# One more column group of forgetting attention is computed inside its loop, and the groups there start and end one third later

## What is computed

```python
def _fox(q, k, v, f_logit, f_bias):
    ...
    log_f = jax.nn.log_sigmoid(f_logit.astype(jnp.float32) + f_bias.astype(jnp.float32))
    cum = jnp.cumsum(log_f, axis=1)
    ...
    def attend(args):
        qb, cq, idx = args
        q_pos = idx * Q_BLOCK + jnp.arange(Q_BLOCK)
        sc = jnp.einsum('bqhd,bkhd->bhqk', qb, k, preferred_element_type=jnp.float32) * scale
        sc = sc + jnp.transpose(cq, (0, 2, 1))[..., None] - cum_k[:, :, None, :]
        sc = jnp.where(k_pos[None, :] <= q_pos[:, None], sc, -jnp.inf)
        p = jax.nn.softmax(sc, axis=-1).astype(v.dtype)
        return jnp.einsum('bhqk,bkhd->bqhd', p, v)
```

## Time and profile before

| | us |
|---|---|
| median of 3 runs (2351.77 to 2354.81) | 2353.89 |
| the profiled execution | 2353.85 |
| its span, first to last instruction | 2352.0 |
| PE busy | 2300.3 (98%) |
| DVE busy | 1443.8 (61%) |
| ScalarE busy | 966.9 (41%) |
| GpSimd busy | 871.3 (37%) |

### The profile page before, as it was taken

How to read it: one execution, slowest core, us unless ns; L and a number is a source line. 1 busy time by engine, 2 the same in 40 slices (tenths; PEclk the granted TensorE clock), 3 DMA queues, 4 the chain that set the end, 5 groups by cost and what they waited for, 6 DMA issues and landing times. The chain is left out here.

```text
span 2352.0 us, 30599 instructions
## 1 busy us (share of the span) xinstructions
PE 2300.3 (98%) x11502; PEld 1934.6 (82%) x11502; DVE 1443.8 (61%) x2287; ACT 966.9 (41%) x1963; POOL 871.3 (37%) x737
## 2 busy tenths in 40 slices
PE   6999999999999999999999999999999999999998
PEld 5887878888888888888998887888888888888887
DVE  6999924955354577775634866243495535457776
ACT  4135544532323245455634655134453232324543
POOL 3000125388787800032112121122338878780002
PEclk9999999999999999999999999999999999999999
DMA  5121124233333368664002100144223323336865
GB/s 156 44 70 65 64 81 134 84 123 106 96 117 103 116 238 284 211 217 118 19 19 70 46 5 19 54 143 144 81 72 117 112 90 116 104 116 242 283 215 194
DMA packets 219445, 275.84 MB, mean 117 GB/s; under 512 B 17243, under 2 KB 144956, under 8 KB 216482
## 3 DMA queue, kind: packets, MB, share of 16 engines
q1 hardware_dynamic: 200594, 210.57, 28.9%
q10 hardware_dynamic: 18704, 63.32, 6.9%
HBM read 205.27 MB, written 68.57 MB: 116 GB/s over the span
## 5 line engine op out<-in xcount | busy, mean ns | idle before, releaser
L494 PE MATMUL P<-ah,wh 128*128 128x512 f32 x1120 | 439.5, 392 | 3.5 <-DVE al L524 2.3
L496 PE MATMUL P<-ah,wl 128*128 128x512 f32 x1120 | 437.0, 390 | 0.0
L495 PE MATMUL P<-al,wh 128*128 128x512 f32 x1120 | 436.8, 390 | 0.0
L494 PE MATMUL P<-wh,ah 128*128 128x512 f32 (+2 forms) x1128 | 425.6, 377 | 0.0
L496 PE MATMUL P<-wh,al 128*128 128x512 f32 (+2 forms) x1128 | 423.3, 375 | 0.0
L495 PE MATMUL P<-wl,ah 128*128 128x512 f32 (+2 forms) x1128 | 422.9, 375 | 0.0
L576 POOL TENSOR_TENSOR stats<-stats,epsc 128x1 f32<-128x1 f32 x78 | 31.0, 397 | 793.7 <-ACT xn L1824 421.0
L494 PEld LDWEIGHTS P<-ah,wh 128*128 128x128 f32 x1120 | 211.0, 188 | 47.5 <-DVE al L524 2.5
L496 PEld LDWEIGHTS P<-ah,wl 128*128 128x128 f32 x1120 | 210.8, 188 | 44.4
L495 PEld LDWEIGHTS P<-al,wh 128*128 128x128 f32 x1120 | 211.0, 188 | 43.1
L496 PEld LDWEIGHTS P<-wh,al 128*128 128x128 f32 x1128 | 212.2, 188 | 36.8
(11 more groups left out here) (357 smaller groups left out, 4292.3 us busy)
## 6 DMA issues: line engine op xcount, KB each, us to landing
rf<-ff_rows SPq DMA_DIRECT2D x154, 256.0 KB, 5.2
stage<-in_w_down_dram SPq DMA_DIRECT2D x110, 256.0 KB, 3.8
ff_rows<-sb ACTq DMA_DIRECT2D x22, 1024.0 KB, 5.0
stage<-in_w_gu_dram SPq DMA_DIRECT2D x44, 512.0 KB, 5.2
stage<-in_w_in_dram SPq DMA_DIRECT2D x22, 512.0 KB, 3.9
stage<-in_w_gate_dram SPq DMA_DIRECT2D x22, 512.0 KB, 4.2
stage<-in_w_up_dram SPq DMA_DIRECT2D x22, 512.0 KB, 5.1
ff_rows<-uo ACTq DMA_DIRECT2D x22, 512.0 KB, 3.0
```

What stands on the lines that cost most here:

```text
L494: e.matmul(out, lh, rh, start=start, stop=False, skip_group_check=onto)
L495: e.matmul(out, lh, rl, start=False, stop=False, skip_group_check=onto)
L496: return e.matmul(out, ll, rh, start=False, stop=stop, skip_group_check=onto)
```

## The change

Group 0 moves from before the loop into steps 0 to 2, and the three others each three steps later, so that the last ends in step 11 in place of step 8. Their splits move with them, and the weights that take over ring slots are sent up to three steps later. All groups use the banks they used.

```diff
@@ narrow_pe
         PE.ends("fqk")
-        fox_later_pe(0, range(8))
@@ narrow_act
         AC.ends("fqk")
-        fox_queries_act(0, 1)
@@ narrow_dve
         DV.ends("fqk")
-        fox_queries_dve(0, 1)
@@ class Fox
-        sends = {1: first["uq"] + 1, 5: first["wo"], 12: first["wo"] + 1, 17: first["wo"] + 2}
+        sends = {4: first["uq"] + 1, 8: first["wo"], 12: first["wo"] + 1, 17: first["wo"] + 2}
@@ filling_pe
-            if it < 9:
-                fox_later_pe(1 + it // 3, range(3 * (it % 3), min(8, 3 * (it % 3) + 3)))
+            if it < 12:
+                fox_later_pe(it // 3, range(3 * (it % 3), min(8, 3 * (it % 3) + 3)))
@@ filling_act
-            if it == 3:
-                fox_queries_act(1, 1)
-            if it in (6, 7, 9, 10):
-                fox_keys_act(it // 3 - 2, 1, it % 3)
+            if it in (3, 6):
+                fox_queries_act(it // 3 - 1, 1)
+            if it in (9, 10, 12, 13):
+                fox_keys_act(it // 3 - 3, 1, it % 3)
@@ filling_dve
-            if it == 3:
-                fox_queries_dve(1, 1)
-            if it in (7, 8, 10, 11):
-                fox_keys_dve((it - 1) // 3 - 2, 1, (it - 1) % 3)
+            if it in (3, 6):
+                fox_queries_dve(it // 3 - 1, 1)
+            if it in (10, 11, 13, 14):
+                fox_keys_dve((it - 1) // 3 - 3, 1, (it - 1) % 3)
```

## The result

The changed kernel takes 2359.20 us, median of ten runs (2356.06 to 2363.05), against 2354.49 us of before (2351.77 to 2355.47): ratio 1.0020, 95% interval 1.0012 to 1.0028. In a second comparison (`e0_again`) it took 2358.32 against 2354.59, 1.0015 (1.0006 to 1.0023). So it is 3.7 to 4.7 us slower, at the edge of the 0.2% that the prediction named as what can be told from no change. The forecast was 2357.0, in a range of 2351.5 to 2361 that also holds the time of before.

A forecast was written before the change was run, and what follows sets the result against it. The prediction took PE, busy 98% of the span, as the bound. Its terms, 0 + 0.8 + 0.9 + 0.6 + 0.2 + 0.6 = +3.1 us on 2353.85, gave 2357.0 us, range 2351.5 to 2361.

The forecast's parts named there:

- Start of step 0: Before the attention loop's first turn: PE idles about 5.4 us without group 0, step 0 starts when it did, 0 us.
- Steps 0 to 8: First nine loop turns: small waits go, -1.13 us, a clock fall after the idle start costs 1.9; sum +0.8 us.
- Steps 9 to 11: Loop turns gaining 24 filler matmuls: 9.3 us without waits against 8.34, so +0.9 us.
- Steps 12 to 16: Last key group's splits land in steps without filler; step 16's scores wait for them, starting 2.3 us late: +0.6 us.
- Steps 16 to 20 and the second half clock: Delay carried to step 20, +0.2 us, and a new clock fall from idle time at steps 14 and 16, 0.6 us.
- Other queues: SyncE's later bias rows, GpSimd's later low halves and DVE's moved split beside one of them: no cost.
- the clock that holds: Rival: neither idle time, at the start or at steps 14 to 16, lowers the clock; +0.6 us, 2354.5; chance 0.14.
- the faster one: Rival: stalls of steps 14 and 16 don't form, PE alone sets steps 0 to 20; 2349.8 to 2351.7 us; chance 0.10.
- The slower one: Rival: full 6.8 us low-clock stretches at the start (3.4 us) and from step 16 (2.5 us); 2360.4; chance 0.24.

The follow-up runs named there:

- e0_again: The changed kernel, unaltered, timed and profiled a second time: 2358.32 us against 2354.59 before, ratio 1.0015.
- e6: Changed kernel with group 0 also computed unused ahead of step 0, plus 6 and 4 unused matmuls at steps 14 and 16: 2353.53 us, ratio 0.9993.
- e5: Changed kernel with 6 unused matmuls ahead of step 14's values and 4 ahead of step 16's scores, start uncovered: 2357.41 us, ratio 1.0011.
- f4_busy_late_again: Changed kernel with unused matmuls in the waits of steps 14 and 16, start uncovered, timed and profiled a second time: 2356.29 us, ratio 1.0010.
- e2_warm: Changed kernel with group 0's 24 matmuls also computed, unused, ahead of step 0: 2353.57 us, ratio 0.9999.
- f1_half_cover: Changed kernel with only 12 unused matmuls ahead of step 0, leaving 2.73 us bare: 2357.79 us, ratio 1.0013.
- after: The changed kernel itself in its first profiled execution, which took 2358.67 us.
- e4_early_splits: Changed kernel with both last-group DVE splits ahead of maximum 14 and step 12's weight sent behind step 15: 2364.55 us, ratio 1.0042.
- f3_stretched_more: Kernel before, group 0 left in place, last group spread to step 11, its splits where the change has them: 2352.56 us, ratio 0.9988.

## Why the prediction was right

Counted from the start of step 0 in two executions of the changed kernel, against the forecast:

- **Start of step 0.** Forecast 5.4 us idle and nothing won; 5.44 us in both, released by DVE's split. Right; it is the step that made the forecast. Covering it takes 3.9 us off the median (`e6` against `e5`) and 2.0 us off the stage in the profiles.
- **Steps 0 to 8, +0.8.** Measured -0.3 and +0.5 (step 9 at 23.9 and 24.6 us, against 24.2). The clock cost 1.5 and 2.2 us in step 0 (3.99 and 4.68 us against 2.52), around the 1.9 taken. Steps 1 to 8 took 1.7 us less, where 1.1 was counted for the waits: PE's busy time in them fell by 0.6 us too, which no run explains. The rule of the Trainium skill ("TensorE: Matmul & The Clock Gate", "The HAM clock gate"), that the throttled state is the default, agrees: the clock fell in all five profiles with 5.44 us of idle time at the start, and in the one with 2.73 us.
- **Steps 9 to 11, +0.9.** 9.41 us in place of 8.34, +1.1, without a wait. Right.
- **Steps 12 to 16, +0.6.** Measured +0.7 (10.5 us against 9.7). The stall at step 14 was 1.51 us (1.4 forecast), the release at step 16 is DVE's last split as forecast. Step 16 came 1.5 and 2.3 us later than before (2.3). PE's wait there was 0.67 and 1.09 us; 2.2 was forecast: the chain was sized well but PE arrived later, having had slow steps in the first execution and another 0.42 us wait for DVE's output in the second.
- **Steps 16 to 20 and the second half clock, +0.8.** This is the term that was sized wrong. They took 12.2 and 11.9 us against 9.7: +2.5 and +2.3. Without half clock (`e5_busy_late`, `f4_busy_late_again`) the same steps took 9.9. I gave the second fall 0.6 us: 3.4 us long, with 0.95 us of it hidden by the wait of step 19, though that wait is 0.58 us. Where the fall came it was 10.2 and 6.8 us long and cost 2.2 and 2.0 up to step 20; 0.4 us of that came back behind it (54.4 us from step 20 to the next attention, 54.8 without the fall). It wasn't there in every kernel with these waits (none in `e2_warm` and `f1_half_cover`), so the average lies below that.
- **Other queues.** No cost, as forecast: the maximum at step 16 did not wait for the bias rows. The moved splits took 1.38 to 1.40 us, also the one at 1312.37, which lay beside GpSimd's low half (2.35 us from 1311.19).

The terms add up to +3.6 and +4.1 us of the stage, against the +3.1 forecast. That this is so near is partly luck: the fillers won more in steps 0 to 8 than was counted, and the second fall cost more. Without either fall (`e2_warm`) step 12 starts 0.7 us earlier than before, the waits of steps 14 and 16 take that back, and step 16 starts at 42.2 us, as before. So in the profiles the change's loss is the price of the two clock falls, and nothing is won in return.

Of the rivals, the clock that holds is refuted at the start; the faster one failed on its stalls. The slower one (2360.4) had the second fall right (2.5 us) and the first too long (3.4 us), and its time is about as near to the measured ones as the forecast's.

Two things stay open. The medians put 2.5 to 4.9 us on the bare start (`f4` against `e6`, the change against `e2`; 3.9 for `e5` against `e6`, which were timed together), the profiles 1.5 to 2.2; the intervals of some 2 us on each median reach from one to the other. Why the late fall came in four profiles (`after`, `e0_again`, `e4_early_splits`, `f3_stretched_more`) and not in `e2_warm` or `f1_half_cover` is not shown. The waits at steps 14 to 16 of these two are those of `e0_again` (1.5, 0.4 and 1.1 us). The start of `f3_stretched_more` was covered, so a fall at the start isn't needed for it. Where in time the waits fell in each execution may decide; that wasn't tried.

## What to carry to other kernels

Work on one engine that ends in the very moment at which a result of another engine arrives is a cover: ask what latency lies under it before counting its time as won. Spread filler toward the idle steps from the work that is already inside the loop, and let its last part end early enough that the work on other engines is done before the step that needs it. When the send of a buffer moves, follow the program of each engine that handles it, since what stands behind it in a queue moves too.

## What was not expected

The half clock outlasted the short waits around it by far. In the changed kernel's first profile it began 1.6 us behind the end of the 1.51 us wait at step 14, and PE was busy 9.44 of the next 10.10 us, all of it at half clock, in steps without filler. In `e5` and `e6` the same steps ran at 1.00.

```profile
1314.60:1324.70 10.10, 9.44 (x43) 8.68 (x41) 7.12 (x21) 5.29 (x13) 0.74 (x2) 0.50 0.15 52
```

At the start, where dense filler followed 5.44 us of standing still, the clock was back within step 0, 4.0 us, in the first execution, and shortly behind it in the second. And the bias of step 0, which DVE now reached earlier, waited 0.52 us for the forget bias rows (1275.41 above); PE did not notice.
